# The moving operand of every split product read, and its result written, from the last column to the first

## The reference

```python
u = rmsnorm(h, mix_norm_w[l])
proj = u @ w_in[l]                                  # 1024 x 8192
...
gu = u @ w_ffn_in[l]                                # 1024 x 5632
h = h + (jax.nn.silu(g) * up) @ w_ffn_out[l]        # 2816 x 1024
...
hid = jax.nn.silu(jnp.einsum('nd,edf->nef', hf, w_gate)) * jnp.einsum('nd,edf->nef', hf, w_up)
out = jnp.einsum('nef,efd->nd', hid, w_down)
```

## Time and profile before

| | |
|---|---|
| median of 3 runs | 1102.29 us (1101.03 to 1104.07) |
| the profiled execution: from its first to its last instruction | 1100.0 us |
| what lies between that span and the median of the runs | 2.3 us |
| TensorE matmuls | busy 1088.2 us, 99% |
| TensorE weight loads | busy 972.6 us, 88% |
| VectorE | busy 730.3 us, 66% |
| ScalarE | busy 625.4 us, 57% |
| HBM | 213.05 MB read, 195 GB/s over the span |
| mean granted TensorE clock | 0.998 of full |

### The profile page before, as it was taken

How to read it: one execution, slowest core, us unless ns; L and a number is a source line. 1 busy time by engine, 2 the same in 40 slices (tenths; PEclk the granted TensorE clock), 3 DMA queues, 4 the chain that set the end, 5 groups by cost and what they waited for, 6 DMA issues and landing times.

```text
span 1100.0 us, 17231 instructions
## 1 busy us (share of the span) xinstructions
PE 1088.2 (99%) x7088; PEld 972.6 (88%) x7088; DVE 730.3 (66%) x817; ACT 625.4 (57%) x751; POOL 48.0 (4%) x42
## 2 busy tenths in 40 slices
PE   9999999999999999999999999999999999999997
PEld 7998889999989999998898768899999978888886
DVE  7844665865765454455875649976444778998895
ACT  7653369664465444444573446855434457877773
POOL 0600100000000000000000000000000000000140
PEclk9999999999999999999999999999999999999999
DMA  8552254654745555554446333253546456999882
GB/s 318 193 192 77 77 192 153 224 191 161 238 164 195 198 194 183 202 192 174 147 167 220 118 115 128 102 192 116 170 154 226 172 211 220 338 379 348 338 343 98
DMA packets 30897, 215.06 MB, mean 196 GB/s; under 512 B 3424, under 2 KB 3680, under 8 KB 5360
## 3 DMA queue, kind: packets, MB, share of 16 engines
q1 hardware_dynamic: 28544, 199.61, 51.3%
q0 software_dynamic: 1872, 13.11, 3.2%
q10 hardware_dynamic: 416, 1.40, 0.3%
HBM read 213.05 MB, written 1.05 MB: 195 GB/s over the span
## 4 chain that ended last, share of the span: by engine, by line
PE 95%; DVE 3%; ACT 1%; issue 0%; DMA 0%; DVEq 0%; ACTq 0%
PE bank L561 29%; PE bank L563 28%; PE bank L562 28%; PE bank L622 2%; PE bank L1033 1%; PE bank L1110 1%; PE bank L955 1%; PE bank L937 1%; DVE wlo L1686 1%; PE bank L682 0%; PE bank L703 0%; PE bank L868 0%; PE bank L1087 0%; PE bank L700 0%; PE bank L864 0%
## 5 line engine op out<-in xcount | busy, mean ns | idle before, releaser
L1686 DVE TENSOR_TENSOR wlo<-raw,whi 128x2048 fp32r<-128x2048 f32 x138 | 317.8, 2307 | 169.4 <-ACT whi L1145 169.2
L1145 ACT ACTIVATE whi<-raw 128x2048 fp32r<-128x2048 f32 (+1 forms) x168 | 319.1, 1906 | 131.7 <-PE bank L563 127.8
L561 PE MATMUL bank<-normedT_hi,whi 128*128 128x256 f32 x640 | 178.2, 278 | 0.0
L562 PE MATMUL bank<-normedT_lo,whi 128*128 128x256 f32 x640 | 177.5, 277 | 0.0
L563 PE MATMUL bank<-normedT_hi,wlo 128*128 128x256 f32 x640 | 177.5, 277 | 0.0
L1145 ACT ACTIVATE buf<-bank 128x512 f32<-128x512 f32 (+5 forms) x147 | 70.9, 526 | 160.3 <-PE bank L563 131.7
L561 PE MATMUL bank<-xT_hi,whi 128*128 128x256 f32 (+1 forms) x448 | 128.0, 286 | 0.8 <-issue 0.8
L563 PE MATMUL bank<-xT_hi,wlo 128*128 128x256 f32 (+1 forms) x448 | 127.6, 285 | 0.0
L562 PE MATMUL bank<-xT_lo,whi 128*128 128x256 f32 (+1 forms) x448 | 127.4, 284 | 0.0
L561 PEld LDWEIGHTS bank<-normedT_hi,whi 128*128 128x128 f32 x640 | 120.1, 188 | 1.0 <-issue 0.6
L563 PEld LDWEIGHTS bank<-normedT_hi,wlo 128*128 128x128 f32 x640 | 120.8, 189 | 0.0
(11 more groups left out here) (405 smaller groups left out, 2266.4 us busy)
## 6 DMA issues: line engine op xcount, KB each, us to landing
raw<-weights_dram SPq DMA_DIRECT2D x168, 1024.0 KB, 5.0
buf<-weights_dram SPq DMA_DIRECT2D x19, 1024.0 KB, 6.9
buf<-x_dram SPq DMA_DIRECT2D x2, 512.0 KB, 4.2
buf<-mem_dram ACTq DMA_DIRECT2D x1, 1024.0 KB, 10.1
out_dram<-buf SPq DMA_DIRECT2D x4, 256.0 KB, 2.7
buf<-final_w_dram POOLq DMA_DIRECT2D x1, 512.0 KB, 4.2
con<-consts_dram SPq DMA_DIRECT2D x1, 486.0 KB, 9.1
buf<-small_w_dram SPq DMA_DIRECT2D x1, 432.0 KB, 11.7
```

The source lines that it names most:

```text
L561: E.matmul(out_, lh, rh, start=start, stop=False)
L562: E.matmul(out_, lh, rl, start=False, stop=False)
L1145: return S.activation(out_, in_, func, **kw)
L1686: V.tensor_tensor(wlo[:, n % SLOTS, :], raw[:, n % SLOTS, :], whi[:, n % SLOTS, :].bitcast(f32), sub).then_inc(piece_split, 1)
```

## The change

Inside `product`, both parts of the moving operand and the output are given as views with their columns reversed. The step along the columns becomes -1, and each access begins at what was its last column. Since the operand and the output are reversed alike, column j of the result still comes from column j of the moving operand and lands at the same address. The stationary operand is read as before.

```diff
             def product(out_, lhs, rhs, start, stop):
 
-                (lh, ll), (rh, rl) = lhs, rhs
+                (lh, ll), (rh, rl) = lhs, tuple(part[:, ::-1] for part in rhs)
+                out_ = out_[:, ::-1]
                 E.matmul(out_, lh, rh, start=start, stop=False)
                 E.matmul(out_, lh, rl, start=False, stop=False)
                 return E.matmul(out_, ll, rh, start=False, stop=stop)
```

## The result

The changed kernel takes 1116.33 us (median of 4 runs, 1115.57 to 1118.82) against 1101.99 us before (4 runs on the same chip): a ratio of 1.0138, with a 95% interval of 1.0122 to 1.0154. It is slower by 15.2 us at that ratio.

A forecast was written before the change was run, and what follows sets the result against it. The prediction took TensorE's matmul rate to bound the kernel. Its three terms, each 0, left 1100.0 us profiled; with 2.3 us by which the runs' median exceeds the span, it forecast 1102.3 us, range 1086 to 1147 us.

The forecast's parts named there:

- no change: Whole kernel: all three terms cost 0, so the time stays at 1102.3 us; chance 0.50.
- the second rival: All products: a stream's start or alignment costs a few ns more, +17 us (1119 us) up to 1165 us; chance 0.20.
- What bounds the kernel: TensorE's matmuls are busy 1088.2 of 1100.0 us; nothing hides a change in their rate, so extra time reaches the end.
- The sum of counts and distances: Split products: matmul counts times distances between starts give 942 us, 86% of the span, the chain's share.
- First term, the read: Moving operand read with step -1: taken as 0; upper ends +201 ns at 512 columns, +100 ns at 256.
- half rate: Every product: neighbouring columns are handled in pairs only at step +1; 819 us more, 1921 us; chance 0.17.
- Second term, the write: Result written with step -1: taken as 0, with the same upper ends as the read; accumulation adds no hazard.
- Third term, where streams start and how they meet: Streams begin at a row's last column while the stationary tile is read: taken as 0, between -17 and +17 us.
- The bound of +17 us: All products in the slow variant: 9 us at 256 columns, 5 us at 512, 3 us for the other 672 matmuls.
- The cover behind the weight load: 256-column products: up to 5 ns of a 10 ns loss could hide behind the weight load, 18 us less.
- higher price: Small loss of 10 ns in each of 6240 matmuls: 62 us, 1165 us; 1147 us with cover.
- plain float32: Reversed fp32r operands carried out as plain float32, two records per matmul: about 3690 us; chance 0.01.

The follow-up runs named there:

- write_only: Kernel before, with only the result written with step -1 and the moving operand read forwards: ratio 1.0003 (0.9991 to 1.0014).
- fours_order: Kernel before, with moving operand and result taken in runs of four columns, runs in backward order, each run forwards: ratio 1.0128 (1.0104 to 1.0151).
- fours_inside: Kernel before, with moving operand and result taken in runs of four columns, runs in forward order, each run backwards: ratio 1.0005 (0.9993 to 1.0017).
- bench_b: Separate bench of 72-matmul blocks after fixed lead-ins, varying stationary width, type and place; forward 256-column blocks ran at 113 or 118 ns between starts.

## Why the prediction was right, and where it was not

The time, 1116.3 us, lies in the range of 1086 to 1147 us, but the likeliest case, no change at 1102.3 us, did not come. What came is the second rival, a small loss, at 0.20; its lower price was +17 us against 15 us measured. The case was allowed for, not forecast.

*What bounds the kernel*: right. The extra nanoseconds of the matmuls went to the end nearly one for one: +15.4 us in the products' distances, +14.4 us in the span. The sum of counts and distances held as well.

*First term, the read*: half rate did not come. The read is backward in every product, and by operands the median distances changed by -3 to +7 ns, not by 100 or 200. The choice of 0 was wrong by the small part that I had put under the third term.

*Second term, the write*: right at 0 (write_only, 1.0003). The prediction gives a PSUM rule of the Trainium skill, that a non-contiguous pattern slows matmuls significantly, and leaves open whether a step of -1 counts as one. By this run it does not, or the rule does not hold for these `fp32r` matmuls. The same page of the Trainium skill, "SBUF — State Buffer", in its section on the DMA port swizzle, names 16-byte lines. The measured border, four words within which direction is free, is of that size; but the page has nothing on the order of lines, and there the loss was. The prediction's reading of it, that four accesses to each line keep the sum as it is, was too narrow: fours_order also makes four accesses to each group of four words, and loses 1.3%.

*Third term, where streams start and how they meet*: this is the step that failed. I took 0 because "turning each stream round should make some quicker and others slower". The turning did not shuffle the variants. It took the quick ones away: 512 columns went from a median distance of 229 ns to 233; `ret` went from 113 to 118 ns, `normedT` from 113 or 114 to 118 or 120, and `lru` stayed at 118. Few matmuls got quicker: the third of each `dsaT` product went from 118 to 115 ns, and the first two lost as much. The loss that I had put at 0 was 15.4 us of distances.

The bound of +17 us was built from these variants (9 + 5 + 3), and the measured shares are 8.0, 7.8 and -0.4 us. The first is near, the 512-column part was larger, since all went to 395 to 397 ns and not to 394, and the 272-column part did not come. That the total is so near is in part luck, as these two errors cancel. My cause for this case, the start of a stream or its alignment, was wrong as well: the loss lies in the order of the groups of four words (fours_order 1.0128, fours_inside 1.0005). The cover behind the weight load, which its higher price gave to the 256-column products, gave no sign of itself: `ret` lost 5 ns, as the 512-column products did. And I put the difference of `ret` and `lru` down to addresses. In the benches the same addresses gave both values; in the kernel itself no run shows what separates the two.

*Half rate and plain float32*: excluded by durations of 282 and 397 ns, against the 380 and 590 ns that they asked for, and by an unchanged number of records.

What stays open: why stepping down from one four-word group to the next costs from 0 to 7 ns per matmul, with the width and the place, in `fp32r`, and none in bfloat16 at the place tried; and what chooses the rhythm and keeps it. The stationary read has a share, since its width and place change the forward time, but no run isolates it; a backward stationary operand was not tried.

## What to carry to other kernels

When TensorE is busy from end to end, a few nanoseconds per matmul are the whole result: read the distance between starts and the spread of durations of equal shapes before taking a reordering as free. If a kernel has quick and slow variants of the same matmul, ask of a change whether it can reach the quick one at all, and don't assume that it will shuffle them. Read `fp32r` moving operands upwards in address from one 16-byte group to the next: with 512 columns that was quicker at two of eight places of the stationary tile, and within 1 ns at five of the others. The order inside the group and the direction of the PSUM write were free here, and the order of 256-byte pieces nearly so.

## What the runs showed of the hardware

- Most blocks of one `fp32r` stream settle into one of a few steady rhythms: 113.3, 117.8 or 120.0 ns for 256 columns, 226.7, 228.9 or 233.3 ns for 512. One and the same block, at the same addresses, ran with 281 and with 276 ns in bench_b.
- The place of the stationary operand, in steps of 8 words, moves a forward 512-column stream between 226.7 and 234 ns; at six of eight places it stands at 233.3 or above, where a backward one usually stands. A bfloat16 stream stood at 215.8 ns in both directions.
- Reading runs of 16 words each backwards, in forward order, is the worst pattern seen: 432 ns for a record and 266.7 ns between starts at 512 columns, and 299 and 133.4 ns at 256.
- With 16 stationary columns a 256-column matmul still came every 118 ns, and with 128 stationary columns one of 128 moving columns every 112 ns.
